# The last tile's order on TensorE: half of an output projection set behind the turn of the convolved rows and the decay products

## What is computed

```python
h = rms_norm(x, norm1_g)
cols = split(h @ w_in)                     # one input projection for three groups of heads
o_a = gla(cols...)                         # gated linear attention, 6 heads
o_b = gated_deltanet(cols...)              # causal conv on q/k/v, silu, l2norm of q and k,
                                           #   per-head decay exp(gcum_i - gcum_j), delta rule, 6 heads
o_c = hgrn2(cols...)                       # 4 heads
x = x + concat([o_a, o_b, o_c]) @ w_out    # the output projection
h2 = rms_norm(x, norm2_g)
x = x + hier_moe(h2)                       # router, then two of 32 SwiGLU experts per token
y = rms_norm(x, final_norm_g)
```

## Time and profile before

| | us |
|---|---|
| median of three runs | 1485.17 |
| lowest, highest | 1482.73, 1488.17 |
| the profiled execution, its time | 1485.2 |
| its span in the trace | 1483.4 |
| TensorE busy | 1290.2 (87% of the span) |
| VectorE, ScalarE, GpSimd busy | 650.4, 408.9, 470.2 |
| mean granted TensorE clock | 0.928 of full speed |

### The profile page before, as it was taken

One profiled execution on the slowest core, in us unless ns is written; L12 is line 12 of the kernel. 1 busy time (PEld: TensorE's weight loads), 2 busy tenths in 40 slices (PEclk: granted clock), 3 DMA queues, 4 the chain that ended last, 5 costly groups with the idle time before them and its releaser, 6 DMA issues. The chain is left out here.

```text
span 1483.4 us, 32235 instructions
## 1 busy us (share of the span) xinstructions
PE 1290.2 (87%) x13766; PEld 991.5 (67%) x13766; DVE 650.4 (44%) x1329; ACT 408.9 (28%) x856; POOL 470.2 (32%) x401
## 2 busy tenths in 40 slices
PE   7898879999999999999999989978745999986960
PEld 6688669879978978988987977767633333332320
DVE  2748735246245336335434625535353322221218
ACT  3134124225223323423422421422100112211113
POOL 1516263154235327236225416424001111111100
PEclk9999889999999999999999999988857999998985
DMA  9967345934833862773682563490078999999977
GB/s 272 253 199 221 103 145 169 280 110 154 274 118 121 257 198 96 236 238 102 200 271 90 161 214 98 130 141 21 7 260 284 363 320 379 374 361 368 367 289 312
DMA packets 273911, 317.28 MB, mean 214 GB/s; under 512 B 15196, under 2 KB 253352, under 8 KB 272336
## 3 DMA queue, kind: packets, MB, share of 16 engines
q1 hardware_dynamic: 261176, 275.81, 59.5%
q10 hardware_dynamic: 5792, 20.78, 4.1%
q0 software_dynamic: 6800, 18.62, 3.3%
HBM read 295.45 MB, written 27.01 MB: 217 GB/s over the span
## 5 line engine op out<-in xcount | busy, mean ns | idle before, releaser
L1521 PE MATMUL psum<-arena 128*128 128x256 f32 (+3 forms) x1536 | 312.8, 358 | 4.4 <-DMA arena<-in_w_in 4.4
L1521 PEld LDWEIGHTS psum<-arena 128*128 128x128 f32 x1536 | 258.7, 195 | 34.9 <-DMA arena<-in_w_in 4.6
L2366 PE MATMUL psum<-arena 128*64 128x512 f32 (+1 forms) x832 | 171.9, 630 | 21.2 <-DMA arena<-in_exp_w 21.2
L1232 DVE COPY_PREDICATED arena<-arena,psum 128x128 f32<-128x128 int32 x280 | 85.2, 304 | 142.6 <-PE psum L1710 135.7
L1517 PE MATMUL psum<-arena 128*128 128x128 f32 x1152 | 140.0, 282 | 4.3 <-DVE arena L1098 4.3
L1517 PEld LDWEIGHTS psum<-arena 128*128 128x128 f32 x1152 | 135.4, 197 | 6.9 <-issue 6.4
L662 POOL TENSOR_TENSOR arena<-arena 128x768 f32<-128x768 f32 (+1 forms) x32 | 59.1, 1846 | 246.6 <-ACT arena L897 246.6
L2366 PEld LDWEIGHTS psum<-arena 128*64 128x64 f32 (+1 forms) x832 | 53.8, 137 | 122.4 <-issue 120.5
L1479 PE MATMUL psum<-arena 64*64 64x64 f32 x3264 | 120.2, 227 | 14.1 <-ACT arena L908 10.3
L1479 PEld LDWEIGHTS psum<-arena 64*64 64x64 f32 x3264 | 108.2, 140 | 31.8 <-ACT arena L908 14.4
L1789 PE MATMUL psum<-arena 128*128 128x256 f32 x512 | 117.5, 389 | 0.8 <-ACT arena L973 0.8
(11 more groups left out here) (402 smaller groups left out, 1956.3 us busy)
## 6 DMA issues: line engine op xcount, KB each, us to landing
arena<-in_w_in SPq DMA_DIRECT2D x96, 1024.0 KB, 6.2
arena<-in_exp_w SPq DMA_DIRECT2D x96, 1024.0 KB, 13.1
arena<-in_w_out SPq DMA_DIRECT2D x32, 1024.0 KB, 5.8
arena<-in_w_in SPq DMA_DIRECT2D x24, 512.0 KB, 5.2
arena<-y_d SPq DMA_DIRECT2D x8, 1024.0 KB, 11.9
arena<-in_x_prompt ACTq DMA_DIRECT2D x15, 512.0 KB, 5.4
arena<-in_w_in SPq DMA_DIRECT2D x8, 576.0 KB, 4.7
arena<-in_w_in SPq DMA_DIRECT2D x8, 560.0 KB, 4.5
```

The costliest lines, as they stand in the source:

```text
L1232: ins = v.copy_predicated(h3(att_b)[:, h:h + 2, :], b3(q_mask[4 * half + j], 2, 64), new)
L1521: ins = mm(b[:, 0:n], hT[:, c, :], w[:, c, 0:n], start=(c == 0), stop=(c == KC - 1))
L2366: ins = mm(bank[2 + q % 2][at:at + width, :], xT[q % 2][:, c, at:at + width], w13[n % NB][:, c, :], start=(c == 0), stop=(c == KC - 1))
```

## The change

In the last tile alone, `project_out(t - 1, 1)` leaves its place behind the transposes of the linear groups and stands behind the decay products: step 3 comes after step 5. The other seven tiles keep their order, and no instruction is added, removed or resized on any engine. The lists of the other four engines stay as they are.

```diff
                 ins.then_inc(step("linT_mm"), 1)
-                if late:
+                if late and not last:
                     project_out(t - 1, 1)
                 done(pe, "cs", t)
                 done(pe, "ex", t)
@@
                 freed(pe, "x2a", t)
                 per_head(bank[2:4], lambda h: blk(gl, h), lambda h: cum).then_inc(step("gam_mm"), 1)
+                if last:
+                    project_out(t - 1, 1)
                 unit(n, spot(n, 8))
                 unit(n, spot(n, 9))
                 done(pe, "kb", t)
```

## The result

The changed kernel takes 1486.69 us as the median of twelve runs, the one before 1482.86 us as the median of twelve beside it: a ratio of 1.003, with an interval from 1.0017 to 1.0043. Measured again on another occasion it was 1.0026 (1.0009 to 1.0043). The forecast of 1479.4 us, 0.39% faster, was wrong: the kernel became slower, by about 0.3%.

What follows compares the result with a forecast made beforehand. The last tile was taken as bound by a dependent chain starting with the turn, which TensorE delayed by 9.32 us of projection. 4.77 + 0.98 = 5.75 us off 1485.2 gave 1479.4 us, range 1476 to 1483.

Steps and rivals of the forecast that it cites:

- The chain: Last tile: first turn starts 8.25 us earlier, `kb` ends at 979.02, third turn starts 4.77 us earlier.
- The clock: Third turn in the last tile: after dense work it should run at 2.4 GHz, 0.98 us more gained.
- The new hole: TensorE ahead of the moved first turn: a 0.8 us wait for `q2`, taken to cost nothing in clock.
- Neither rival on the clock: Clock falls in the new hole: 1481.4 to 1482.9, chance 0.15; low clock returns behind the moved chain: 1481.5, 0.10.
- `residual(6, 1)`: VectorE's addition in the last tile ends at 982.3; ScalarE asks for it only at 985.06, so no delay.
- SyncE's queue: Last output-weight load and small stores behind it go 3.6 us later; costed at nothing, 3.6 us without cover.
- the sum: Whole kernel: 4.77 + 0.98 = 5.75 us off 1485.2 us, giving 1479.4 us, 0.39%.
- The third: Turn held by something besides `q2`, or barrier by SyncE's stores; hole only changes place: 1484.5 to 1486, chance 0.06.
- The one for the slower side: Clock falls in the new hole, stays low for the whole half projection: 9.9 us cost, 1490 us, chance 0.04.
- The sign that the text gave for being wrong: Among the signs of being wrong: recurrence levels from L1646 on take over 2 us longer than before.

Runs made afterwards that it cites:

- first experiment: Nine 4-byte stores of the convolution state left out: of the changed kernel, 1477.8 us, ratio 0.9958; of the kernel before, 1483.9 us, 1.0005.

## Why the prediction was wrong, step by step

- **The chain, right.** The turn began at 969.49 (forecast 970.7 - 1.29 = 969.41) and `kb` ended at 977.78 (979.02 - 1.29 = 977.73). The third turn came 4.98 us earlier for 4.77, L875 5.96 for 5.75, L1816 5.97 for 5.75.
- **The clock, right.** The new hole was 0.88 us and the clock stayed at 1.00 across it; the third turn took 1.20 us and not 2.19. Neither rival on the clock came about there.
- **`residual(6, 1)`, right.** VectorE's L1313 waits for ScalarE, not for the residual.
- **SyncE's queue, the step that failed.** "The last one moves with the end of the half, 3.6 us later, and so do the small stores queued behind it ... I cost this at nothing; with that cover gone it would be 3.6 us." The move is right: in the two traces the issue goes from 979.67 to 981.77, relative to the tile 2.10 + 1.29 = 3.4 us later. The price was taken from those who wait for the stores by a semaphore, and there is nobody. It is paid by TensorE, which stalls while they are under way: without them (first experiment) or with rows in their place there is no stall. Its fetch, which starts at 996 to 999 in the changed kernels that keep the gain, started at 1008.26 and took 3.85 us. The hole costs 8.0 us in the profile, where nothing was put down.
- **What the sum never named.** The gain itself moved ScalarE's stores of x2 and h2 some 6 us forward, into the small stores that the same change moved 3.4 us back. Before, they were mostly one behind the other. With these two stores moved away the gain is kept (1477.84 us). A step that becomes faster starts its DMAs sooner too, and these were not in the list of moved queues.
- **The rivals.** All four were mechanisms of TensorE, its clock, or the barrier. The third comes nearest: it names SyncE's stores and a hole that only changes its place. But it lets the stores hold the barrier, which they do not, and ends at 1486, below the 1486.69 measured. The one for the slower side (the clock low for the whole half projection) did not happen; the slower outcome came by a mechanism that no rival held. The sign that the text gave for being wrong, levels from L1646 on that are over 2 us longer, is what is seen; its cause is not the clock, which falls to 0.50 at 1004 and stays low through the hole.

What stays open: why the large stores draw out the small ones; what delays the start of a fetch and TensorE's signals while the small stores are under way, and which of the two comes first; what makes the short pieces in the kernels with the stores ahead or held; and the 5.8 us between the fetch's end and TensorE's next product in the old order with held stores. That the 4-byte stores cause the stalls is shown by leaving them out, by storing rows, and by moving them in the old order. That it is the fetch through which they do it fits the long holes of the changed kernel, and only in part the rest.

## What to carry to other kernels

A transfer that nobody waits for is not free: ask which other queues are at work beside it, and count the queues of instructions among them. Stores of single elements should be turned into rows on the chip, or kept away from stretches in which an engine runs through many short instructions. Where a trace shows idle time with no releaser, look at the instruction queues in that stretch, at when a fetch starts and not only at how long it takes, and at engines behind it that were released late.

## What the runs showed of the hardware

A packet of q8, 0.02 MB, taken here for a fetch of TensorE's instructions, took 0.88 to 1.38 us in the trace of before between 945 and 1070. In the stalls of the changed kernel it took 3.85, 3.75, 1.46 and 2.98 us and started 6 to 17 us later in the tile than in the versions without a stall; in the old order with held stores it took 5.0 us. The same 13.8 KB of stores in rows of 512 bytes left it at 0.96 us. TensorE's signals came up to 5.4 us late in the changed kernel's first profile. And where TensorE stood still for 4.0 to 10.3 us at once, it did so behind one product, the first of 32 alike, in both orders.
